# Differential attention takes a filling unit of projection products at every step in place of every second step

## What is computed

```
h = rms_norm(x, ln1_g[l]);  proj = h @ w_in[l]            # 256 x 6048 columns
a_q,a_k,a_v, b_q,b_k,b_v, c_cq,c_ckv,c_kr, gate_logits = split(proj)
y_a = grouped-query attention, axial rotary, heads of 64
y_b = differential attention:
      sc = einsum('bqhcd,bshcd->bhcqs', q, k)             # 8 heads, c = 2 parts of 32
      p  = softmax(sc);  p = p[:, :, 0] - lam * p[:, :, 1]
      o  = einsum('bhqs,bshe->bqhe', p, v);  rms_norm(o) per head * (1 - lambda_init)
y_c = latent attention of rms_norm(c_cq) @ w_uq and rms_norm(c_ckv) @ w_ukv
merged = sum_n sigmoid(gate_n) * (y_n @ w_branch[l][n]);  x = x + merged @ w_out[l]
x = x + relu(rms_norm(x, ln2_g[l]) @ w_ff1[l])^2 @ w_ff2[l]
```

## Time and profile before

| | |
|---|---|
| runs of the kernel before, median | 2555.1 us |
| the profiled execution's own time | 2549.77 us |
| its span, first to last instruction | 2548.0 us |
| PE busy | 2498.7 us, 98% |
| DVE busy | 1885.1 us, 74% |
| ACT busy | 1495.8 us, 59% |
| GpSimd (POOL) busy | 0.2 us |
| mean granted TensorE clock | 0.996 of full speed |
| read from device memory | 581.79 MB, mean 229 GB/s |

### The profile page before, as it was taken

How to read it: one execution, slowest core, us unless ns; L and a number is a source line. 1 busy time by engine, 2 the same in 40 slices (tenths; PEclk the granted TensorE clock), 3 DMA queues, 4 the chain that set the end, 5 groups by cost and what they waited for, 6 DMA issues and landing times.

```text
span 2548.0 us, 38641 instructions
## 1 busy us (share of the span) xinstructions
PE 2498.7 (98%) x16734; PEld 2231.6 (88%) x16734; DVE 1885.1 (74%) x1665; ACT 1495.8 (59%) x1520; POOL 0.2 (0%) x4
## 2 busy tenths in 40 slices
PE   9999999999999999999999999999999999999998
PEld 8889999877888888888888887998899999899998
DVE  7765556858888888888888888657775575777655
ACT  6463336457777777777777777446553455565433
POOL 0000000000000000000000000000000000000000
PEclk9999999999999999999999999999999999999999
DMA  6335554325999999999999998433345553243552
GB/s 247 133 116 183 182 183 148 133 84 190 364 358 362 359 363 355 363 349 367 352 364 357 364 356 313 173 132 116 133 166 188 178 180 133 101 162 122 188 190 83
DMA packets 83520, 585.38 MB, mean 230 GB/s; under 512 B 9420, under 2 KB 11308, under 8 KB 12820
## 3 DMA queue, kind: packets, MB, share of 16 engines
q1 hardware_dynamic: 83348, 582.87, 61.8%
HBM read 581.79 MB, written 1.05 MB: 229 GB/s over the span
## 4 chain that ended last, share of the span: by engine, by line
PE 88%; DVE 7%; ACT 3%; issue 1%; DMA 0%; DVEq 0%; ACTq 0%
PE PS L1798 87%; DVE wlo L1053 2%; ACT whi L555 1%; PE PS L2331 1%; PE PS L2012 1%; ACT pb L667 1%; DVE stat L1200 1%; DVE pb L1214 1%; DVE hT L1099 0%; ACT pt L684 0%; DVE xT L1378 0%; DVE hlo L1105 0%; DVE pb L1218 0%; DVE hlo L1069 0%; DMA raw<-in_ws 0%
## 5 line engine op out<-in xcount | busy, mean ns | idle before, releaser
L1053 DVE TENSOR_TENSOR wlo<-raw,whi 128x2048 fp32r<-128x2048 f32 x550 | 1257.9, 2290 | 361.7 <-ACT whi L555 352.9
L555 ACT ACTIVATE whi<-raw 128x2048 fp32r<-128x2048 f32 x550 | 1052.0, 1914 | 310.3 <-PE PS L1798 273.4
L1798 PE MATMUL PS<-hhi,whi 128*128 128x256 f32 x1984 | 573.1, 289 | 10.0 <-DVE hlo L1105 2.6
L1798 PE MATMUL PS<-hlo,whi 128*128 128x256 f32 x1984 | 562.4, 283 | 0.0
L1798 PE MATMUL PS<-hhi,wlo 128*128 128x256 f32 x1984 | 562.2, 283 | 0.0
L1798 PEld LDWEIGHTS PS<-hhi,whi 128*128 128x128 f32 x1984 | 381.3, 192 | 24.5 <-issue 16.3
L1798 PEld LDWEIGHTS PS<-hlo,whi 128*128 128x128 f32 x1984 | 381.4, 192 | 0.7 <-issue 0.5
L1798 PEld LDWEIGHTS PS<-hhi,wlo 128*128 128x128 f32 x1984 | 381.3, 192 | 0.0
L1798 PE MATMUL PS<-whi,xghi 128*128 128x512 f32 x896 | 359.9, 402 | 1.2 <-DVE wlo L1053 1.1
L1798 PE MATMUL PS<-whi,xglo 128*128 128x512 f32 x896 | 355.0, 396 | 0.0
L1798 PE MATMUL PS<-wlo,xghi 128*128 128x512 f32 x896 | 354.9, 396 | 0.0
(11 more groups left out here) (374 smaller groups left out, 3574.8 us busy)
## 6 DMA issues: line engine op xcount, KB each, us to landing
raw<-in_wm SPq DMA_DIRECT2D x336, 1024.0 KB, 5.6
raw<-in_ws SPq DMA_DIRECT2D x214, 1024.0 KB, 4.8
xT<-in_xT SPq DMA_DIRECT2D x4, 256.0 KB, 6.8
bsum<-in_bsum SPq DMA_DIRECT2D x1, 1024.0 KB
out_T<-hT SPq DMA_DIRECT2D x4, 256.0 KB, 2.5
lmask<-in_lmask SPq DMA_DIRECT2D x1, 512.0 KB
onehot_in<-in_onehot SPq DMA_DIRECT2D x1, 288.0 KB
lbw<-in_lbw SPq DMA_DIRECT2D x1, 256.0 KB
```

The source lines that it names most:

```text
L555: act.activation(whi[s % SPLIT][:], raw[s % RAW][:], ACT.Copy).then_inc(hi_ready, 1)
L1053: dve.tensor_tensor(wlo[s % SPLIT][:], raw[s % RAW][:], whi[s % SPLIT][:].bitcast(F32), ALU.subtract).then_inc(lo_ready, 1)
L1798: return pe.matmul(out, a, b, start=start, stop=stop, skip_group_check=True)
```

## The change

The argument `fill_every=2` is taken from the call of differential attention in all three programs, so the default 1 holds and every step asks for a filling unit. Nothing else is edited; the products, their operands and the order of the units in the stream stay the same.

```
@@ scalar_program, second_mixer @@
-                attention(diff_heads(), pb2, pt2, fill_every=2)
+                attention(diff_heads(), pb2, pt2)
@@ vector_program, second_mixer @@
-                attention(diff_heads(), pb2, fill_every=2)
+                attention(diff_heads(), pb2)
```

## The result

The changed kernel takes 2580.96 us (median of 4 runs, 2579.28 to 2583.54), the kernel before 2554.97 us in the same comparison: a ratio of 1.0109, 95% interval 1.0097 to 1.0122, so slower by about 26 us by the medians and 27.8 us by the ratio; the further experiments are compared by their ratios. The forecast was 2578.8 us.

The account below looks back on a forecast made before the run. PE bounds the kernel (88% of the span), through its work and idle time. Norm gaps 21.2 plus table load 0.4 less attention's 4.0 give +17.6 us; clock adds 6.1: 2555.1 + 23.7 = 2578.8 us, range 2570 to 2589.

Parts of the forecast that it names:

- Which units move: Filling list: 9 units left at differential attention, all taken there, none in the norms; 4 move per layer, 8 in all.
- Waits removed in attention: Differential attention: PE waits of 1.52 and twice 0.55 us go, 0.34 stays, 0.78 is new; 4.0 us saved in all.
- Idle time in the norms: Two head norms: uncovered gaps of 1.6, 3.1, 2.6, 3.1 us; with edges 10.6 us per layer, 21.2 in all.
- The table load: ACT's 1.28 us load for the norms' root runs beside PE's sums and adds nothing; the skill page would add 1.6 us.
- The small terms: Start of latent attention: ACT's exponential table load sticks out, 0.2 us per layer (bounds 0 and 1.3).
- Clock: Norms and branch product: second sums doubled (2.3 us) plus one spell (1.45 us), 3.8 us per layer, 7.6 in all.
- the spell that layer 1 had already: Behind layer 1's norms: existing half-clock time worth 1.45 us, subtracted against double counting, leaving 6.1 us net for the clock.
- +34 us: Whole kernel: slowdown if, by the skill page, every gap of the new norms works against the clock, nearer the upper bound.
- Sum: Whole kernel: 17.6 us at full clock plus 6.1 us for the clock, +23.7 us.
- Rival 1: TensorE in the norms: clock stays at 2.4 GHz, so only +17.6 us, time 2572.7 us; chance 0.20.
- Rival 2: Differential attention: doesn't become PE-bound, softmax chain through DVE and ACT holds it, 6 us more, 2584.8 us; chance 0.13.
- Rival 3: Filling list: doesn't run out, norms stay covered, -4.0 us, 2551.1 us or no measurable change; chance 0.05.

Follow-up runs that it names:

- The even pairs in the kernel after: Changed kernel, with attention scores of jobs n and n + 1 issued together at even n: 2577.94 us, ratio 1.0094 to the kernel before.
- the run with dummies: Changed kernel plus unused 128x128 products into idle bank 7 in the norms' four gaps: 2569.93 us, ratio 1.0074 to the kernel before.
- the kernel with bare norms: Kernel before, attention untouched, no filling units in the two norms, four leftover units in a row after them: 2594.42 us, ratio 1.0173.
- the two with one norm bare: Kernel before with seven units in differential attention, two in one norm, none in the other: y norm bare 2569.83 us, cc norm bare 2572.03 us.
- even pairs in the kernel before: Kernel before, with row maxima and scores of jobs n and n + 1 taken together at even n: 2552.79 us, ratio 1.0002.

## Why the prediction was right

- **Which units move.** Nine in attention, none in the norms, as counted from the list.
- **Waits removed in attention.** Right to 0.01 us each: 0.78 and 0.34 are the only ones left. The stretch was forecast at 70.3 us and took 70.90. A term was overlooked: at steps 1 and 2 of the kernel before, with no unit between them, 16 score products took 1.09 us, and with a unit between them they take 1.06 us twice, 1.0 us more. The four units took about 0.5 us less than the 23.8 counted for them, which leaves the 0.6. The even pairs in the kernel after show the same work disappear again.
- **Idle time in the norms.** Forecast 1.6, 3.1, 2.6, 3.1; measured 1.65, 3.16, 2.42, 3.09. The third is 2.73 at full clock, as the run with dummies showed, and the 2.6 was worked out for full clock. At full clock the stretch was to be 18.0 us and is 18.18 with dummies. The table load did run beside the sums, which end at 1785.66, and the root follows them and not the load, as ACT's timeline of the kernel after shows:

```profile
1783.65 1.28 ACT L634 ACT_TABLE_LOAD   x1
1785.70 0.46 ACT L634 ACTIVATE rs<-PS,epsc 16x256 f32<-16x256 f32 x1 [0.77 <-PE PS L1798]
```

  "ScalarE: Activation LUTs" of the Trainium skill (section "What ACT_TABLE_LOAD costs") adds a drain of 1.38 us to the load of 1.28 us. By an estimate from these two figures the root could not have started before 1786.3; the trace has it at 1785.70 and disagrees with the page.
- **The small terms.** The first gate of latent attention waits 0.96 us instead of 0.83, so 0.13 us for the table of the exponentials against 0.2.
- **Clock.** This was the guess: 3.8 us per layer, 7.6 in all; measured against the dummies 4.7 and 2.95, 7.65 in all. That the sum fits is luck: no layer took 3.8, and the parts differ. In layer 0 it was 2.1 us for the sums over `cc`, 1.3 for the two spreads less what the third gap gave back, and 1.3 for the branch product and what follows, where 2.3 and 1.45 had been put down and nothing for the spreads. The 1.45 us subtracted for the spell that layer 1 had already were too many. Where the branch product is slow, the wait of 0.9 us for the next unit's low part disappears (latent products 18.2 us before, 17.0 after), so the spell of 1.5 us there costs about 0.4 us net. What was cited from "TensorE: Matmul & The Clock Gate" of the Trainium skill (section "Part 1: The HAM clock gate"), that the clock falls when the array idles, agrees with this trace, where PEclk is 0.50 from about the end of the second gap; the size set beside it, +34 us, was too dear.
- **Sum.** Forecast 17.6 at full clock and 6.1 for the clock, 23.7; measured by stretches 18.7 and 7.65, 26.4. The 2.7 us between them are attention (1.1, the scores), the spell of layer 1 counted too dear (1.1) and 0.2 us per norm stretch (0.4).

Rival 1 (clock stays) is what the kernel with dummies shows, +19 us in place of the +17.6 that it gave. Rival 2 didn't happen: no step of attention waits for the softmax chain beyond the 0.34 us that stayed. Rival 3 is excluded by the count of units.

What stays open: which idle patterns bring the clock down. Ten layers in the traces have a wait of 1.45 or 1.52 us in differential attention: the kernel before, the kernel with bare norms, the two with one norm bare, and even pairs in the kernel before. In nine of them PEclk fell to 0.50 within some 2 us of its end, and not in layer 0 of the kernel before. In the ten layers whose longest wait there was 0.78 us or less, attention had no spell. No run varied the length of a wait alone.

## What to carry to other kernels

Work that fills gaps is a budget: before one place is given more of it, count who is served last from the list and price that place's chain with nothing in it. Here 4 units covered 10.3 us of links in the norms and, moved, shortened attention by 1.4 to 1.6 us. A wait inside a stage that is nearly balanced can be one engine's order, and cheaper to cure there: one reduction taken ahead shortened attention by 2.9 to 3.1 us.

## What the runs showed of the hardware

- TensorE ran at 1.2 GHz (PEclk 0.50) behind stretches in which it waited, and this slowed narrow and wide products alike: the sums over `cc` 4.42 against 2.33 us, the branch product 8.2 against 5.8 us. Dummy products in the gaps, which nobody reads, kept it at 2.4 GHz (PEclk 1.00) and gave back 8.9 us of 27.8.
- A wait of 1.45 or 1.52 us in attention was followed by PEclk 0.50 in nine layers of ten: mix 1.47 for 1.09 us, scores 2.08 for 1.13 us directly behind one.
- Score products on 32 rows each, of two jobs whose operands lie in different rows, ran side by side when issued back to back: 16 in 1.09 us, 8 in 1.06 us.
- An ACT table load of 1.28 us ran beside PE's sums while ACT had to wait for them anyway, and the root started 0.04 us behind the sums (1785.66 to 1785.70), so the load cost nothing.
